# Straight and crossed TensorE quadrants alternating in the chunk inverses of a hybrid decoder kernel

## The chip, the core and the metric

The kernel runs on one core of a Trainium2 chip. The core has TensorE (matrix products; PE in the profile, its weight loads PEld), VectorE (DVE), ScalarE (ACT), GpSimd (POOL) and the DMA queues. Matrix products land in eight banks of PSUM, each 128 partitions by 512 float32. Each time is the device time of one execution in microseconds, and the kernel's time is the median of its runs.

## The reference, cut to what matters

The kernel computes one inference step of a decoder trunk of four layers, for a prompt of 256 tokens and 8 sample sequences of 4 tokens. Layers 0 and 3 have an RWKV-7 time mixer as their token mixer, layer 1 has differential attention, and layer 2 a gated DeltaNet (GDN). In front of each mixer and behind it stands a feed-forward half, which takes most of the time. The mixer's core is this recurrence over the tokens, for 16 heads with 64x64 states:

```python
def step(S, inp):
    r_t, w_t, k_t, v_t, a_t, b_t = inp
    sa = jnp.einsum('bhvk,bhk->bhv', S, a_t)
    S = S * w_t[:, :, None, :] + sa[..., None] * b_t[:, :, None, :] + v_t[..., None] * k_t[:, :, None, :]
    return S, jnp.einsum('bhvk,bhk->bhv', S, r_t)
S, o = lax.scan(step, S0.astype(f32), seq)
```

## The kernel before

The recurrence is not run token by token. The prompt's 256 tokens are cut into four chunks of 64 (c = 0 to 3), and what the tokens of a chunk do to each other is solved by a triangular 64x64 matrix of each head, which has to be inverted. The inverse is built on a ladder of five steps, l = 1 to 5 (LADDER is 6), that doubles the size of the inverted blocks. Each step has two products: Y = (matNT) times the inverse so far, which VectorE multiplies with a mask of 0 and 1 into Yc, and X = (transpose of the inverse) times Yc, which ScalarE copies out as the next inverse. The last step gives the transposed inverse (XTfin) and swaps the operands.

Sixteen heads lie as eight head pairs: the even head of a pair on partitions 0 to 63 (HALVES[0]), the odd one on 64 to 127 (HALVES[1]). A product of 64x64 matrices takes one quadrant of TensorE's array; which one is set by the partitions that it reads and those that it writes. Before, each head reads and writes its own half, so only the two straight quadrants work (0 to 0 and 64 to 64). The head pairs are worked in two groups g of four, q = 0 to 3. Each float32 product stands as two instructions in the trace, so one half of a step (Y or X of both groups) is 8 pairs x 2 heads x 2 = 32 recorded instructions.

What follows what is written out by hand: each engine has its own list of instructions, in the order of the code, and waits on semaphores.

- TensorE (chunk_inverse): Y of g0 and g1 (L1434 in the trace) after inv_ready; then other work of the mixer (spread_inverse L1378 in chunk 0, chunk_output L1505 to L1513 of the chunk before, products of the sample sequences); X of g0 and g1 (L1461, in the last step L1463) after invy_ready and invt_ready; then more such work (transposes L1538 in chunk 0, L1554 and L1562 to L1566 in chunk 2, L1577 and L1585 in chunk 3).
- VectorE (L3128 and around): for each group the transpose of the inverse (turned_inverse, L3072, 32x32 blocks of a 128x256 tile), then the mask (L3111). Beside it stand copies of the samples' states (L3057, L3065), the chunk's outputs (chunk_output, L3207 to L3209) and sample products (L3094 to L3098, L3123 to L3125).
- ScalarE: inverse_out (L2457), for each group one copy from the bank. In step 1 (chunk 1: step 2), behind these, chunk_matrix copies the chunk's matrices out of MK_BANK (L2538, L2540), and counts chunk_a_ready.

The banks, before: X and Y of group g share bank XY_BANK[g] = 0, 1 (X in columns 0 to 255, Y in 256 to 511), and the last step writes XT_BANK = 2, 3. From chunk 1 on, MK_BANK is (2, 3) and MB_BANK (0, 1). So TensorE waits for chunk_a_ready only in front of the last X, which reuses banks 2 and 3.

The gated DeltaNet layer has an inverse of its own (gdn_inverse, L2057 and L2086), in which from step 1 on the products of one pair go to straight and crossed quadrants in turn (L2086), and those of L2057 use two quadrants.

Of the kernel before, what the change touches and what calls it, by code (L numbers as in the profile page):

```python
# [28 lines left out]
LADDER = 6  # L29
# [114 lines left out]
def program(nc, t, stages):  # L144
    f32 = mybir.dt.float32
    ALU = mybir.AluOpType
# [3 lines left out]
    with ctx:  # L150
# [255 lines left out]
        V_BANK, KB_BANK = (0, 4), ((1, 2), (6, 7))  # L406
        MK_BANK, MB_BANK = ((6, 7), (2, 3)), ((3, 0), (0, 1))
        own_inverse = work[:, XM0_, :, :].rearrange("p c n -> p (c n)")
# [7 lines left out]
        X_BANK, Y_BANK, RU_BANK, OS_BANK = (3, 1), (0, 2), (4, 5), (6, 7)  # L416
        XY_BANK, XT_BANK = (0, 1), (2, 3)
        GDN_INVERSES = 2 * (2 * (LADDER - 1) + 2) + 2
# [165 lines left out]
        def out_lo_count(s, w=None, x=None):  # L584

            return out_before(s) + (x + 1 if w is None else CH + w + 1)

        def out_before(s):

            return split_before[s] + {"rwkv": 6, "attn": 3, "gdn": 2}[stages[s][0]] * CH  # L590
# [379 lines left out]
        def _(pe):  # L970
# [430 lines left out]
            def chunk_matrices(c, g):  # L1401
# [10 lines left out]
                last.then_inc(chunk_a_raw, 1)  # L1412

            def chunk_inverse(c, meanwhile, behind):

# [4 lines left out]
                for l in range(1, LADDER):  # L1420
                    for g in range(2):
                        if c or l > 1:
                            after(inv_ready)
                        elif g == 0:
                            after(inv_ready, 2)
                        if l == 1:
                            if c:
                                after(chunk_a_ready)
                            elif g == 0:
                                after(chunk_a_ready, 2)  # L1430
                        for q in range(4):
                            hp = 4 * g + q
                            for r in HALVES:
                                last = nc.tensor.matmul(bank[XY_BANK[g]][r, 256 + 64 * q:320 + 64 * q], matNT[r, hp, :],  # L1434
                                                        invX[r, hp, :], start=True, stop=True)
                        last.then_inc(invy_raw, 1)
# [11 lines left out]
                    for g in range(2):  # L1448
                        after(invy_ready)
                        if l == LADDER - 1 and g == 0:  # L1450
                            after(invt_ready, 2)
                        elif 1 < l < LADDER - 1:
                            after(invt_ready)
                        if c and l == LADDER - 1:
                            after(chunk_a_ready)
                        for q in range(4):
                            hp = 4 * g + q
                            for r in HALVES:
                                y, xt = Yc[r, hp, :], invXT[r, hp, :]
                                if l < LADDER - 1:  # L1460
                                    last = nc.tensor.matmul(bank[XY_BANK[g]][r, 64 * q:64 * q + 64], xt, y, start=True, stop=True)  # L1461
                                else:
                                    last = nc.tensor.matmul(bank[XT_BANK[g]][r, 64 * q:64 * q + 64], y, xt, start=True, stop=True)  # L1463
                        last.then_inc(inv_raw, 1)
# [737 lines left out]
        def _(act):  # L2202
# [130 lines left out]
            def rwkv(s, j):  # L2333
# [121 lines left out]

                def inverse_out(g, dst, ready, banks_):
                    return nc.scalar.copy(dst[:, 4 * g:4 * g + 4], bank[banks_[g]][:, 0:256].rearrange("p (c n) -> p c n", n=64)).then_inc(ready, 1)  # L2457

                for c in range(NCHUNK):
# [22 lines left out]
                    for l in range(1, LADDER - 1):  # L2482
                        if c == 3 and l == 4:
                            new_states(2)
                        for g in range(2):
                            after(inv_raw)
                            inverse_out(g, invX, inv_ready, XY_BANK)
                        if c == 1 and l == 1:
# [25 lines left out]
                    for g in range(2):  # L2514
                        after(inv_raw)
                        inverse_out(g, XTfin, invt_ready, XT_BANK)
                    if c == 1:
# [321 lines left out]
        def _(dve):  # L2839
# [45 lines left out]
            def rwkv(s, j):  # L2885
# [184 lines left out]
                def turned_inverse(g, out, src):  # L3070
                    heads = slice(4 * g, 4 * g + 4)
                    return V.transpose(out[:, heads].rearrange("p c n -> p (c n)"), src[:, heads].rearrange("p c n -> p (c n)"))  # L3072

                for c in range(NCHUNK):
                    f = min(c, 1)
# [9 lines left out]
                    for l in range(1, LADDER):  # L3085
# [18 lines left out]
                        for g in range(2):  # L3104
                            if l > 1:
                                if l == 2 and g == 0:
                                    after(inv_ready, 2 + (GDN_INVERSES if j and c == 0 else 0))
                                after(inv_ready)
                                turned_inverse(g, invXT, invX).then_inc(invt_ready, 1)
                            after(invy_raw)  # L3110
                            TT(Yc[:, 4 * g:4 * g + 4], bank[XY_BANK[g]][:, 256:512].rearrange("p (c n) -> p c n", n=64),  # L3111
                               each4(const(f"block{l}")), ALU.mult).then_inc(invy_ready, 1)
                        if c and l in (2, 3):
# [828 lines left out]
```

## Time and profile before

| | us |
|---|---|
| median of 3 runs (lowest, highest) | 2791.18 (2789.64, 2796.64) |
| the profiled execution's own time | 2788.76 |
| its span, from first to last instruction | 2787.1 |
| TensorE busy | 2730.9 |
| VectorE busy | 1669.9 |
| ScalarE busy | 1238.3 |
| GpSimd busy | 286.0 |

The granted TensorE clock is 0.995 of full speed over the span. The chain of work that ended last is 90% TensorE; the three lines of the feed-forward and projection products alone are 24% each. The ladder's lines L1434, L1461 and L1463 are in the two stretches of the recurrent mixers, at 354 to 486 us and at 2396 to 2528 us. A row of the timeline gives the start, the time from the first start to the last end of the merged instructions, and the engine, line and operation; in brackets stands the idle time in front and what ended it.

### The profile page before, as it was taken

What the parts mean: (1) busy time and instruction counts of PE and PEld (TensorE: products, weight loads), DVE (VectorE), ACT (ScalarE), POOL (GpSimd) and SP (SyncE); (2) the same over time, 40 slices, a digit from 0 to 9 for tenths busy, and PEclk for the clock granted to TensorE, in tenths of its full rate; (3) what the DMA queues carried; (4) which work ended last, traced back from release to release, by engine and by line L of the source; (5) the groups of instructions that cost most, each with busy time, mean ns of one, the idle gap of its engine ahead of it and who ended that gap; (6) DMA issues with size and microseconds to landing.
All of it is one profiled execution on the core that took longest, in us unless ns stands there. A gap on an engine that the chain in (4) does not pass through costs nothing.

```text
span 2787.1 us, 60635 instructions
## 1 busy us (share of the span) xinstructions
PE 2730.9 (98%) x26617; PEld 2579.8 (93%) x26617; DVE 1669.9 (60%) x2529; ACT 1238.3 (44%) x1988; POOL 286.0 (10%) x343
## 2 busy tenths in 40 slices
PE   9999999999999999999999999999999999999999
PEld 8997988999999986999999998789999979788999
DVE  5646866665565546665565594546556558866653
ACT  5435643544444334543443473234344356445443
POOL 2001023000000102000000121410000010122001
PEclk9999999999999999999999999999999999999999
DMA  9444401653653655444653443254455353206442
GB/s 283 132 146 137 139 33 37 190 163 128 198 169 127 245 183 201 143 149 142 187 168 125 155 163 109 69 177 146 144 188 166 127 169 121 63 4 185 151 134 79
DMA packets 351611, 402.47 MB, mean 144 GB/s; under 512 B 31290, under 2 KB 306127, under 8 KB 350989
## 3 DMA queue, kind: packets, MB, share of 16 engines
q1 hardware_dynamic: 340448, 361.73, 40.4%
q0 software_dynamic: 10976, 38.07, 4.4%
q8 instruction: 139, 2.28, 0.3%
q14 instruction: 48, 0.39, 0.0%
HBM read 385.19 MB, written 14.57 MB: 143 GB/s over the span
## 4 chain that ended last, share of the span: by engine, by line
PE 90%; DVE 6%; ACT 2%; issue 1%; DMA 1%; SPq 0%; POOL 0%; DVEq 0%; ACTq 0%; POOLq 0%
PE banks L1018 24%; PE banks L1020 24%; PE banks L1019 24%; PE banks L1461 1%; PE banks L1434 1%; PE banks L1161 1%; PE banks L1008 1%; PE banks L1632 1%; PE banks L1069 1%; PE banks L1585 1%; PE banks L1014 1%; PE banks L1948 1%; DVE ring_lo L2941 1%; PE banks L1409 0%; DVE h L2856 0%
## 5 line engine op out<-in xcount | busy, mean ns | idle before, releaser
L2871 DVE TENSOR_TENSOR w_lo<-ring,w_hi 128x2048 fp32r<-128x2048 f32 (+1 forms) x303 | 609.1, 2010 | 409.5 <-ACT w_hi L2320 409.5
L1018 PE MATMUL banks<-h_hi,w_hi 128*128 128x288 f32 x2816 | 836.9, 297 | 1.1 <-DVE h_lo L2863 0.8
L1019 PE MATMUL banks<-h_hi,w_lo 128*128 128x288 f32 x2816 | 831.5, 295 | 0.0
L1020 PE MATMUL banks<-h_lo,w_hi 128*128 128x288 f32 x2816 | 828.5, 294 | 0.0
L2320 ACT CAST w_hi<-ring 128x2048 fp32r<-128x2048 f32 (+1 forms) x303 | 509.5, 1682 | 573.2 <-PE banks L1020 545.1
L1018 PEld LDWEIGHTS banks<-h_hi,w_hi 128*128 128x128 f32 x2816 | 528.2, 188 | 3.4 <-DVE h_lo L2863 1.9
L1020 PEld LDWEIGHTS banks<-h_lo,w_hi 128*128 128x128 f32 x2816 | 531.0, 189 | 0.0
L1019 PEld LDWEIGHTS banks<-h_hi,w_lo 128*128 128x128 f32 x2816 | 529.1, 188 | 0.4
L1018 PE MATMUL banks<-hid_hi,w_hi 128*128 128x288 f32 x1408 | 416.1, 296 | 0.0
L1019 PE MATMUL banks<-hid_hi,w_lo 128*128 128x288 f32 x1408 | 415.4, 295 | 0.0
L1020 PE MATMUL banks<-hid_lo,w_hi 128*128 128x288 f32 x1408 | 414.3, 294 | 0.0
L1020 PEld LDWEIGHTS banks<-hid_lo,w_hi 128*128 128x128 f32 x1408 | 265.1, 188 | 0.0
L1019 PEld LDWEIGHTS banks<-hid_hi,w_lo 128*128 128x128 f32 x1408 | 264.3, 188 | 0.0
L1018 PEld LDWEIGHTS banks<-hid_hi,w_hi 128*128 128x128 f32 x1408 | 263.8, 187 | 0.0
L2819 ACT CAST hid_hi<-work 128x288 fp32r<-128x288 f32 x176 | 76.2, 433 | 397.9 <-DVE work L3615 397.9
L3671 POOL TENSOR_TENSOR h<-h 128x288 f32<-128x288 f32 x65 | 78.8, 1215 | 1508.8 <-ACT h L2249 902.8
L3607 DVE TENSOR_TENSOR work<-banks,rinv 128x288 f32<-128x288 f32 x176 | 80.5, 457 | 174.0 <-PE banks L1020 174.0
L3617 DVE TENSOR_TENSOR hid_lo<-work,hid_hi 128x288 fp32r<-128x288 f32 x176 | 80.7, 458 | 87.8 <-ACT hid_hi L2819 87.8
L1019 PE MATMUL banks<-h_hi,ring_lo 128*128 128x288 f32 x448 | 132.6, 296 | 0.0
L1019 PEld LDWEIGHTS banks<-h_hi,ring_lo 128*128 128x128 f32 x448 | 84.9, 189 | 0.1
L3630 DVE SCALAR_TENSOR_TENSOR x<-banks,x 128x288 f32<-128x288 f32 x64 | 29.3, 457 | 85.8 <-PE banks L1020 85.8
L3615 DVE TENSOR_TENSOR work<-work 128x288 f32<-128x288 f32 x176 | 79.5, 452 | 1.8 <-ACT work L2817 1.8
(607 smaller groups left out, 4239.9 us busy)
## 6 DMA issues: line engine op xcount, KB each, us to landing
ring<-in_ffn_w_gate SPq DMA_DIRECT2D x87, 1024.0 KB, 5.5
ring<-in_ffn_w_up SPq DMA_DIRECT2D x87, 1024.0 KB, 8.0
ring<-in_ffn_w_down SPq DMA_DIRECT2D x64, 768.0 KB, 4.6
ring<-in_ffn_w_down SPq DMA_DIRECT2D x64, 640.0 KB, 5.8
ring<-in_rwkv_w_rkv SPq DMA_DIRECT2D x24, 1024.0 KB, 6.5
ring<-in_gdn_w_in SPq DMA_DIRECT2D x16, 1024.0 KB, 7.4
ring<-in_attn_w_qkv SPq DMA_DIRECT2D x12, 1024.0 KB, 7.4
ring<-in_rwkv_w_o SPq DMA_DIRECT2D x8, 1024.0 KB, 6.3
```

The lines of the kernel that those rows point to most:

```text
L1008: last = nc.tensor.matmul(bank[at][:, 0:NT], ones[:, :], h[:, c, :], start=(c == 5), stop=(c == 7))
L1018: nc.tensor.matmul(out, w_hi_k, x_hi_k, start=start, stop=False)
L1019: nc.tensor.matmul(out, w_lo_k, x_hi_k, start=False, stop=False)
L1020: return nc.tensor.matmul(out, w_hi_k, x_lo_k, start=False, stop=stop)
L2320: nc.scalar.copy(w_hi[e][:, 0:k, :], raw).then_inc(w_hi_ready, 1)
L2819: nc.scalar.copy(hid_hi[:, 2 * u + e, :], prod[:, e, :]).then_inc(act_hi_ready, 1)
L2871: nc.vector.tensor_tensor(w_lo[e][:, 0:k, :], raw, w_hi[e][:, 0:k, :], ALU.subtract).then_inc(w_lo_ready, 1)
L3607: nc.vector.tensor_tensor(silu[:, e, :], bank[2 * e][:, 0:NT], rinv[:, :], ALU.mult)
L3615: nc.vector.tensor_tensor(prod[:, e, :], silu[:, e, :], prod[:, e, :], ALU.mult).then_inc(prod_ready, 1)
L3617: nc.vector.tensor_tensor(hid_lo[:, f, :], prod[:, e, :], hid_hi[:, f, :], ALU.subtract).then_inc(act_lo_ready, 1)
L3630: nc.vector.scalar_tensor_tensor(x[:, c, :], bank[4 + c % 4][:, 0:NT], 0.5, x[:, c, :], ALU.mult, ALU.add).then_inc(x_updated, 1)
L3671: nc.gpsimd.tensor_tensor(h[:, c, :], h[:, c, :], h[:, other, :], ALU.add).then_inc(presummed, 1)
```

## The change

Half of the head pairs of a group (q = 2 and 3) now run on the crossed quadrants: head e of the pair reads its half and writes the other one in Y; in X it is turned back. They go to banks of their own, CROSS_BANK = 1, 3, while q = 0 and 1 stay in XY_BANK = 0, 2, and the order is q = 0, 2, 1, 3, straight and crossed in turn. It starts at step 2 (chunk 1: step 3, first_crossed); step 1 stays straight in bank XY_BANK[g]. The transposes must follow: for a crossed step each group has three (turned_halves), one for the two straight pairs over all partitions and two for the crossed pairs, from half 0 to half 1 and back. MK_BANK and MB_BANK of the later chunks move, and chunk_a_ready is waited for in front of the first crossed Y.

```diff
-        MK_BANK, MB_BANK = ((6, 7), (2, 3)), ((3, 0), (0, 1))
+        MK_BANK, MB_BANK = ((6, 7), (1, 3)), ((3, 0), (0, 2))
...
-        XY_BANK, XT_BANK = (0, 1), (2, 3)
+        XY_BANK, CROSS_BANK = (0, 2), (1, 3)
+        QUAD_ORDER = (0, 2, 1, 3)
...
+        def first_crossed(c):
+            return 3 if c == 1 else 2
+        def ladder_read(c, l, g, at):
+            if l < first_crossed(c):
+                return bank[XY_BANK[g]][:, at:at + 256].rearrange("p (b n) -> p b n", b=2)
+            return banks[:, XY_BANK[g]:CROSS_BANK[g] + 1, at:at + 128]
...
+            def ladder_out(c, l, g, q):
+                if l < first_crossed(c):
+                    return 0, bank[XY_BANK[g]][:, 64 * q:]
+                return q // 2, bank[(XY_BANK, CROSS_BANK)[q // 2][g]][:, 64 * (q % 2):]
...
+                        elif c and l == first_crossed(c):
+                            after(chunk_a_ready)
-                        for q in range(4):
+                        for q in QUAD_ORDER:
                             hp = 4 * g + q
-                            for r in HALVES:
-                                last = nc.tensor.matmul(bank[XY_BANK[g]][r, 256 + 64 * q:320 + 64 * q], matNT[r, hp, :],
-                                                        invX[r, hp, :], start=True, stop=True)
+                            for i, r in enumerate(HALVES):
+                                at, out = ladder_out(c, l, g, q)
+                                last = nc.tensor.matmul(out[HALVES[i ^ at], 256:320], matNT[r, hp, :], invX[r, hp, :], start=True, stop=True)
...
-                        if c and l == LADDER - 1:
-                            after(chunk_a_ready)
...
+                                y, xt = Yc[HALVES[i ^ at], hp, :], invXT[HALVES[i ^ at], hp, :]
                                 if l < LADDER - 1:
-                                    last = nc.tensor.matmul(bank[XY_BANK[g]][r, 64 * q:64 * q + 64], xt, y, start=True, stop=True)
+                                    last = nc.tensor.matmul(out[r, 0:64], xt, y, start=True, stop=True)
...
+                def turned_halves(g):
+                    own, other = slice(4 * g, 4 * g + 2), slice(4 * g + 2, 4 * g + 4)
+                    flat = lambda a: a.rearrange("p c n -> p (c n)")
+                    V.transpose(flat(invXT[:, own]), flat(invX[:, own]))
+                    for i in range(2):
+                        last = V.transpose(flat(invXT[HALVES[1 - i], other]), flat(invX[HALVES[i], other]))
+                    return last
...
-                                turned_inverse(g, invXT, invX).then_inc(invt_ready, 1)
+                                (turned_inverse(g, invXT, invX) if l < first_crossed(c) else turned_halves(g)).then_inc(invt_ready, 1)
```

The copy of ScalarE and the mask of VectorE read through ladder_read, with as many elements as before.

On VectorE, step 2 of chunk 0, this stood in a row before (the first copy is of the samples' states, STREAM_TRANSPOSE the ladder's transpose, the operation into h the mask):

```order
279 L3057 COPY ring<-banks 128x512 [waits seq_t_raw]
280 L3072 STREAM_TRANSPOSE work<-work 128x256 [waits inv_ready]
281 L3111 TENSOR_TENSOR h<-banks,consts 128x256 [waits invy_raw]
282 L3072 STREAM_TRANSPOSE work<-work 128x256 [waits inv_ready]
283 L3111 TENSOR_TENSOR h<-banks,consts 128x256 [waits invy_raw]
```

And this stands there now:

```order
279 L3075 COPY ring<-banks 128x512 [waits seq_t_raw]
280 L3095 STREAM_TRANSPOSE work<-work 128x128 [waits inv_ready]
281 L3097 STREAM_TRANSPOSE work<-work 64x128 x2
282 L3137 TENSOR_TENSOR h<-banks,consts 128x256 [waits invy_raw]
283 L3095 STREAM_TRANSPOSE work<-work 128x128 [waits inv_ready]
284 L3097 STREAM_TRANSPOSE work<-work 64x128 x2
285 L3137 TENSOR_TENSOR h<-banks,consts 128x256 [waits invy_raw]
```

Each transpose has become three, and the mask stands behind the third.

On TensorE, chunk 2, the end of step 1 (L1554, products of the samples) and Y of step 2 before (ahead of the fillers L1505; some semaphores share a number, so a wait can have another user's name):

```order
1374 L1554 MATMUL banks<-work 64x64 [waits seq_a_ready,pageT_ready_act]
1375 L1554 MATMUL banks<-work 64x64 x15
1376 L1434 MATMUL banks<-work 64x64 [waits inv_ready]
1377 L1434 MATMUL banks<-work 64x64 x7
1378 L1434 MATMUL banks<-work 64x64 [waits inv_ready]
1379 L1434 MATMUL banks<-work 64x64 x7
```

And now:

```order
1374 L1572 MATMUL banks<-work 64x64 [waits seq_a_ready,pageT_ready_act]
1375 L1572 MATMUL banks<-work 64x64 x15
1376 L1454 MATMUL banks<-work 64x64 [waits chunk_a_ready,inv_ready]
1377 L1454 MATMUL banks<-work 64x64 x7
1378 L1454 MATMUL banks<-work 64x64 [waits chunk_a_ready,inv_ready]
1379 L1454 MATMUL banks<-work 64x64 x7
```

The instructions are as many as before and in the same place; both groups now wait for chunk_a_ready, which has gone from the last X.

## Rows read from the trace of the kernel before

**Rows 1.** The page's head.
```profile
span 2787.1 us, 60635 instructions
```

**Rows 2.** Windows of both mixers: busy us by engine, clock, DMA.
```profile
353.96:486.24 132.28, 125.62 (x3307) 109.96 (x3306) 83.79 (x182) 56.45 (x146) 40.86 (x37) 1.00 0.12 27
2395.80:2528.10 132.30, 125.64 (x3307) 109.94 (x3306) 83.81 (x182) 56.48 (x146) 40.85 (x37) 1.00 0.12 27
```

**Rows 3.** Timeline, TensorE, chunk 0: start us, length us, instruction.
```profile
366.33 1.09 PE L1538 MATMUL banks<-consts,ring 128*128 128x128 f32 x8
369.49 1.15 PE L1461 MATMUL banks<-h,work 64*64 64x64 f32 x32
370.57 1.09 PE L1538 MATMUL banks<-consts,ring 128*128 128x128 f32 x8
...
380.34 1.15 PE L1463 MATMUL banks<-work,h 64*64 64x64 f32 x32 [0.50 <-DVE work L3072]
```

**Rows 4.** Timeline, VectorE, chunk 0, step 2.
```profile
367.46 0.69 DVE L3057 COPY ring<-banks 128x512 f32<-128x512 f32 x1 [0.82 <-PE banks L1538]
368.07 0.43 DVE L3072 STREAM_TRANSPOSE work<-work 128x256 f32<-128x256 f32 x1
368.43 0.38 DVE L3111 TENSOR_TENSOR h<-banks,consts 128x256 f32<-128x256 f32 x1
368.74 0.42 DVE L3072 STREAM_TRANSPOSE work<-work 128x256 f32<-128x256 f32 x1
369.09 0.38 DVE L3111 TENSOR_TENSOR h<-banks,consts 128x256 f32<-128x256 f32 x1
```

**Rows 5.** Timeline, TensorE, the GDN inverse.
```profile
1718.82 1.16 PE L2086 MATMUL banks<-work 64*64 64x64 f32 x64
1720.01 1.15 PE L2057 MATMUL banks<-work 64*64 64x64 f32 x32
```

**Rows 6.** VectorE group of one shape: count, busy us, mean ns, idle before.
```profile
L3551 DVE TENSOR_TENSOR work<-work,banks 128x128 f32<-128x128 f32 x2 | 0.5, 284 | 0.0
```

**Rows 7.** Timeline, VectorE, copies between partition halves.
```profile
316.92 0.19 DVE L3013 COPY kinv<-work 128x32 f32<-128x32 f32 x1
317.02 0.77 DVE L3017 COPY kinv<-work 64x32 f32<-64x32 f32 x4
```

**Rows 8.** Timeline, ScalarE and TensorE, chunk 2, step 2.
```profile
422.37 1.10 PE L1434 MATMUL banks<-work 64*64 64x64 f32 x32
422.68 0.37 ACT L2540 COPY work<-banks 128x256 f32<-128x256 f32 x1
...
423.70 0.37 ACT L2540 COPY work<-banks 128x256 f32<-128x256 f32 x1
```

**Rows 9.** Timeline, all engines, chunk 1.
```profile
400.06 2.36 POOL L3691 TENSOR_TENSOR work<-work,consts 128x1024 f32<-128x1024 f32 x1
400.84 1.87 DVE L3209 TENSOR_TENSOR h<-h,kinv 128x256 f32<-128x256 f32 x1
...
404.76 0.67 DVE L3123 TENSOR_TENSOR work<-work,consts 128x512 f32<-128x512 f32 x1
...
410.19 1.10 PE L1463 MATMUL banks<-work,h 64*64 64x64 f32 x32
```

**Rows 10.** Timeline, VectorE and TensorE, chunk 2.
```profile
427.94 0.68 DVE L3094 TENSOR_TENSOR work<-banks,work 128x512 f32<-128x512 f32 x1
...
430.51 1.10 PE L1554 MATMUL banks<-work 64*64 64x64 f32 x32
...
433.66 1.34 PE L1461 MATMUL banks<-h,work 64*64 64x64 f32 x32 [1.12 <-DVE h L3111]
...
438.42 1.15 PE L1463 MATMUL banks<-work,h 64*64 64x64 f32 x32 [0.62 <-DVE h L3111]
```

**Rows 11.** Timeline, VectorE and TensorE, chunk 3.
```profile
453.24 0.69 DVE L3065 COPY ring<-banks 128x512 f32<-128x512 f32 x1 [2.74 <-PE banks L1585]
...
459.38 1.15 PE L1461 MATMUL banks<-h,work 64*64 64x64 f32 x32
```

More of the change, by code:

```diff
@@ L1453, in chunk_inverse @@
                             after(invt_ready)
-                        if c and l == LADDER - 1:
-                            after(chunk_a_ready)
-                        for q in range(4):
+                        for q in QUAD_ORDER:
                             hp = 4 * g + q
-                            for r in HALVES:
-                                y, xt = Yc[r, hp, :], invXT[r, hp, :]
+                            for i, r in enumerate(HALVES):
+                                at, out = ladder_out(c, l, g, q)
+                                y, xt = Yc[HALVES[i ^ at], hp, :], invXT[HALVES[i ^ at], hp, :]
                                 if l < LADDER - 1:
-                                    last = nc.tensor.matmul(bank[XY_BANK[g]][r, 64 * q:64 * q + 64], xt, y, start=True, stop=True)
+                                    last = nc.tensor.matmul(out[r, 0:64], xt, y, start=True, stop=True)
                                 else:
-                                    last = nc.tensor.matmul(bank[XT_BANK[g]][r, 64 * q:64 * q + 64], y, xt, start=True, stop=True)
+                                    last = nc.tensor.matmul(out[r, 0:64], y, xt, start=True, stop=True)
                         last.then_inc(inv_raw, 1)
@@ L2454, in new_states, with inverse_out @@
                     nc.scalar.copy(dst[:, 0], bank[4 + 2 * (p // 2)][:, :].rearrange("p (q b k) -> p b q k", q=2, b=4)).then_inc(seq_new_ready, 1)
-                def inverse_out(g, dst, ready, banks_):
-                    return nc.scalar.copy(dst[:, 4 * g:4 * g + 4], bank[banks_[g]][:, 0:256].rearrange("p (c n) -> p c n", n=64)).then_inc(ready, 1)
+                def inverse_out(c, l, g, dst, ready):
+                    return nc.scalar.copy(dst[:, 4 * g:4 * g + 4].rearrange("p (b q) n -> p b (q n)", b=2), ladder_read(c, l, g, 0)).then_inc(ready, 1)
                 for c in range(NCHUNK):
@@ L2486, in rwkv @@
                             after(inv_raw)
-                            inverse_out(g, invX, inv_ready, XY_BANK)
+                            inverse_out(c, l, g, invX, inv_ready)
                         if c == 1 and l == 1:
@@ L2515, in rwkv @@
                         after(inv_raw)
-                        inverse_out(g, XTfin, invt_ready, XT_BANK)
+                        inverse_out(c, LADDER - 1, g, XTfin, invt_ready)
                     if c == 1:
@@ L3108, in rwkv @@
                                 after(inv_ready)
-                                turned_inverse(g, invXT, invX).then_inc(invt_ready, 1)
+                                (turned_inverse(g, invXT, invX) if l < first_crossed(c) else turned_halves(g)).then_inc(invt_ready, 1)
                             after(invy_raw)
-                            TT(Yc[:, 4 * g:4 * g + 4], bank[XY_BANK[g]][:, 256:512].rearrange("p (c n) -> p c n", n=64),
-                               each4(const(f"block{l}")), ALU.mult).then_inc(invy_ready, 1)
+                            TT(Yc[:, 4 * g:4 * g + 4].rearrange("p (b q) n -> p b q n", b=2),
+                               ladder_read(c, l, g, 256).rearrange("p b (q n) -> p b q n", n=64),
+                               each4(const(f"block{l}")).rearrange("p (b q) n -> p b q n", b=2), ALU.mult).then_inc(invy_ready, 1)
                         if c and l in (2, 3):
```

## The prediction

> **What bounds the kernel now.** I read four things in this order: the span and the windows of the two recurrent mixers, the timeline of one ladder step with its waits, one place elsewhere in the kernel that already uses crossed quadrants, and the rows that price narrow VectorE instructions. The reader is to see this. The profiled execution took 2788.76 us with a span of 2787.1 us [rows 1]; it is 2.4 us below the median of the runs, 2791.18, so I make the sum on 2788.76 and add 2.4 at the end. TensorE is busy for 2730.9 us of it. The change touches only the two mixer stretches of 132.3 us each [rows 2]; in each, TensorE is busy for 125.6 us and VectorE for 83.8 us, at full clock. The two stretches agree within 0.02 us, so I work one and double it. Outside them TensorE goes on bound by its own products, so a shift in a mixer should reach the end whole.
>
> Names used below: a ladder step l has two halves on TensorE, Y (the products of matNT and X) and X (the products of Yc and the transpose). Each half is 8 head pairs in two groups g0, g1, 32 recorded instructions. VectorE does for each group a transpose T and then a mask M; ScalarE copies X out. "Last start" is when the last instruction of a half starts.
>
> One step of chunk 0 shows who ends last. TensorE runs transposes L1538, Y, spread L1378, X, transposes again: from 366.33 to 370.57, 4.24 us, with no idle time in front of any of them [rows 3]. VectorE runs copy L3057, T, M, T, M from 367.46, and its last M starts at 369.09 [rows 4]; X starts right behind the end of that M, 369.47. So TensorE bounds, with VectorE's chain only just hidden. That is the cover which the change spends.
>
> **Part 1: TensorE, quicker halves.** A half of 32 instructions takes 1.15 us from first start to last end, straight quadrants only [rows 3]. The GDN inverse has halves in which straight and crossed pairs alternate: 64 instructions took 1.16 us, beside 1.15 us for its own 32-instruction halves that use two quadrants [rows 5]. So twice the instructions fit in the same time. A recorded instruction lasts 0.218 us and the first after a wait 0.267 us, so the 32 starts spread over 0.93 us, 0.058 us for two; with four quadrants it is 0.058 us for four, 0.47 us in all. A crossed half saves 0.47 us. Chunks 0, 2 and 3 have 4 crossed steps (8 halves), chunk 1 has 3 (6 halves): 30 halves, 14.0 us in a mixer, if nothing else is late. The ScalarE copies and the masks keep their sizes (they read two banks in place of one): I cost that at nothing, since the element counts do not change; if the step from bank to bank took 0.01 us, the 22 masks that my chains have on the path in a mixer would make 0.4 us in both.
>
> **Part 2: VectorE, three transposes in place of one.** For each group of a crossed step one 128x256 transpose becomes one 128x128 and two 64x128. No row shows a transpose of that width. Bounds: at 128 columns a mask-like operation takes 0.284 us, against 0.384 for the same kind at 256 columns [rows 4, 6], 0.10 to 0.13 less, so a narrow transpose is about 0.31 us from 0.43; at the most, it costs as much as the wide one. At the least, consecutive operations overlap by 0.07 us (T to M starts 0.36 apart at a duration of 0.43 [rows 4]), so 0.24 apart.
>
> What decides is whether they overlap. The second reads half 0 and writes half 1, the third the reverse, and M goes back to half 0. Just such a sequence stands in the trace [rows 7]: L3013 takes 0.19 us and the next operation starts 0.10 us behind its start, but the four copies of L3017, each going to or from other partition halves, take 0.77 us together. Less one duration of 0.19, that is 0.19 to 0.20 us from start to start: they do not overlap at all. So I take 0.32 us from start to start three times, 0.96 us from T to M, where 0.36 stood: 0.60 us more for a group, 1.2 us for a step. Bounds for T to M: 3 x 0.24 = 0.72 us and 3 x 0.45 = 1.35 us.
>
> The Trainium skill has a rule for this ("VectorE: DVE Perf Modes", section Two Vector instructions with no wait between them): an instruction whose input or output starts in another 32-partition quadrant than the last one's is held until every earlier Vector instruction has finished. It speaks against this change; by it all three steps (second, third, M) are held, and the trace agrees at L3017. Without it T to M would be 0.72 us.
>
> **Part 3: a wait moved forward.** Crossed results go to banks 1 and 3, where the chunk's own matrices lie until ScalarE has copied them. So chunk_a_ready is now waited for at the first crossed step, and not at the last. In chunk 2 that is l=2: Y started at 422.37, but ScalarE ends the copies of g0 at 423.05 and of g1 at 424.07 [rows 8]. g1 starts at 424.12 and its last instruction at 424.35, in place of 423.30: 1.05 us later where 0.47 earlier was to be had, a cost of 1.5. Queued behind it on TensorE is all the rest. In chunk 1 (l=3) the same order of copies costs 1.2 us. In chunk 3 other matmuls stand between, and the copies are done in time: nothing.
>
> **The sum by chunk, start to start.** From the start of the first T to the last start of X there are 0.96 + 0.31 + 0.96 to the second M, 0.42 for that M (it no longer overlaps), and 0.33 until the last instruction of g1's X: 2.98 us. Where VectorE decides, I follow this chain.
>
> - Chunk 0. At l=2 T starts at 368.07 as now; X's last start is 371.05, where it is 370.42 (369.49 + 0.93): +0.6. Then a loop: 0.15 to L1538, 1.16 to L3057, 0.61 to T, 2.98: 4.9 us, against 4.24: +0.7 for l=3. Step 4 now takes 3.8 (it has a shorter spread): +1.1. Step 5: 0.8 us of VectorE work stands between M and T, and it takes 3.35 from last start to last start, where X (380.34 [rows 3]) shows 2.8: +0.6. Together +3.0.
> - Chunk 1. VectorE's L3209 lasts until 402.71 beside GpSimd work that ends at 402.42 [rows 9], and this end stays. T at 402.7; M of g0 waits for Y to 403.8, second M at 405.1, then 0.31 and three products of 0.64 (L3123 [rows 9] and its two like), T 407.3, X's last start 410.3. It is 411.1 now (410.19 + 0.88): -0.8. The 2.8 us of part 1 have paid for the wait and for this.
> - Chunk 2. L3094 at 427.94 [rows 10] stays too, as L3209 before it again ends with GpSimd's work. T at 428.55, X's last start 431.53, where it is 430.46, just ahead of L1554 at 430.51: +1.1. L1554 follows 1.1 later; 1.15 us behind its start L3097, 1.21 us for it and the next, then 2.98: X's last start 436.9 against 434.8 (433.66 + 1.12): +2.2. The fillers and the copy before the last T take 2.45 as now, X's last start 442.4 against 439.35 (438.42 + 0.93): +3.0.
> - Chunk 3. T at 453.85 (L3065 at 453.24 + 0.61 [rows 11]), X 456.8; chunk_output's three operations follow the mask (1.4 us), T at 457.5, X's last start 460.5 against 460.31 (459.38 + 0.93 [rows 11]): +0.2. The last four halves have long matmuls between them and save 0.47 each, 1.9, less 0.4 us where g1 waits for its mask at l=4: -1.3.
>
> Together 3.0 - 0.8 + 3.0 - 1.3 = +3.9 us a mixer, +7.8 us in two. 2788.8 + 7.8 + 2.4 = 2799.0 us. The clock stays at its upper level (2.4 GHz, 1.00 granted): no wait that I add is longer than 1.5 us, and idle times of 1.1 us stand in chunk 2 now [rows 10] at full clock.
>
> **Rivals.**
>
> (a) The transposes overlap after all (0.24 apart, 0.72 from T to M). For it: a transpose and the mask behind it overlap now [rows 4]. Against it: the copies of [rows 7]. The same chains give +0.6, -1.4, +1.1 and -2.9: -2.6 us a mixer, 2786 us.
>
> (b) A narrow transpose costs what the wide one costs (1.35 from T to M). That is 0.78 us more in each of about 11 steps that VectorE then bounds: 8.6 us a mixer more, 3.9 + 8.6 = 12.5, twice, 2816 us. For it: no row has the width. Against it: all other kinds get cheaper with fewer columns.
>
> (c) TensorE remains the bound, and VectorE's growth hides in its idle 48 us of each stretch. 14.0 us less the moved wait of 2.7: 11.3 a mixer, 2769 us, faster. For it: the shares in [rows 2]. Against it: T, M, T, M stand in a row between two halves, and there the cover is 0 in chunk 0. It needs T to M at no more than about 0.5 us.
>
> (d) The quadrants do not overlap here, so the change does not do what it says: halves stay at 1.15 us and VectorE's part comes on top. About 7.8 us a mixer of the saved halves that my sum uses would be gone: 11.7 twice, 2814 us. Against it: [rows 5], with the same sizes and the same alternation.
>
> **How the numbers follow.** About 8.4 us, 0.3%, is what a measurement of this kernel can tell from no change. My forecast of 7.8 lies at that border: its own range is 2793 to 2804, as the 0.31 us of a narrow transpose is uncertain by 0.02, which is worth 2.5 us in all, and the chains by some 3. It has 0.62 (0.31 slower, 0.31 same); (a) 0.13, within 0.3%; (b) 0.10, slower; (c) 0.08, faster; (d) 0.03, slower; 0.04 for what I have not named, faster for the most part. Slower 0.44, same 0.44, faster 0.12. The range reaches below (a) and nearly to (b): 2782 to 2815.
>
> **What would show it.** Right: 64*64 halves of the ladder with last starts 0.44 behind the first where nothing is waited for; transposes of about 0.31 us whose starts lie 0.32 apart; T to M near 0.96; TensorE idle of 0.5 to 1.5 us before X in chunks 0 and 2, put down to the masks; chunk 0 longer by 3 us, chunk 3 shorter by 1.3; Y at the first crossed step of chunk 2 waiting for ScalarE's L2540 copies. Wrong: transposes that overlap, or of 0.43 us; idle time before X on TensorE no longer than now; or a difference that arises outside the two stretches.

## The result and the profile after

The changed kernel takes 2810.53 us (median of 4 runs, 2809.76 to 2814.87), beside 2790.41 us for the kernel before in the same comparison: the ratio is 1.007, with a 95% interval of 1.0058 to 1.0082. That is 20.1 us more. The forecast was 2799.0 us, 7.8 us more. The sign was right and the time lies inside the range of 2782 to 2815, but the difference is 2.6 times the one worked out. The page of the profiled execution (2809.76 us) begins:

```profile
span 2808.1 us, 60761 instructions
```

All of it arises in the two mixer stretches. These are their windows, cut at the same instructions as [rows 2] (span, busy us of PE, PEld, DVE, ACT and POOL, granted clock, DMA share, GB/s):

```profile
353.83:496.35 142.52, 120.91 (x3306) 102.91 (x3306) 97.00 (x241) 56.07 (x145) 40.69 (x37) 0.95 0.11 25
2406.49:2550.11 143.62, 121.46 (x3306) 103.93 (x3306) 96.98 (x241) 56.07 (x145) 40.69 (x37) 0.94 0.10 24
```

They are 10.24 and 11.32 us longer than the 132.28 and 132.30 of before, 21.6 in all; the profiled executions differ by 21.0. VectorE is busy for 13.2 us more in each (97.00 against 83.79), as three transposes stand for one. And the last columns have something new: the clock is at 0.95 and 0.94 of full speed, where it was at 1.00.

Step 2 of chunk 0 on VectorE, which answers to [rows 4] (start us, length us, instruction):

```profile
367.33 0.69 DVE L3075 COPY ring<-banks 128x512 f32<-128x512 f32 x1 [0.81 <-PE banks L1556]
367.94 0.30 DVE L3095 STREAM_TRANSPOSE work<-work 128x128 f32<-128x128 f32 x1
368.26 0.63 DVE L3097 STREAM_TRANSPOSE work<-work 64x128 f32<-64x128 f32 x2
368.92 0.43 DVE L3137 TENSOR_TENSOR h<-banks,consts 128x256 f32<-128x256 f32 x1
369.26 0.30 DVE L3095 STREAM_TRANSPOSE work<-work 128x128 f32<-128x128 f32 x1
369.57 0.62 DVE L3097 STREAM_TRANSPOSE work<-work 64x128 f32<-64x128 f32 x2
370.23 0.42 DVE L3137 TENSOR_TENSOR h<-banks,consts 128x256 f32<-128x256 f32 x1
```

From the start of T to the start of M it is 0.98 us, where 0.36 stood. The same step on TensorE, for [rows 3]:

```profile
366.20 1.09 PE L1556 MATMUL banks<-consts,ring 128*128 128x128 f32 x8
367.23 0.69 PE L1454 MATMUL banks<-work 64*64 64x64 f32 x32
367.85 1.12 PE L1389 MATMUL banks<-work,consts 128*128 128x512 f32 x2
369.40 0.46 PE L1479 MATMUL banks<-h,work 64*64 64x64 f32 x16 [0.42 <-DVE h L3137]
370.71 0.46 PE L1479 MATMUL banks<-h,work 64*64 64x64 f32 x16 [0.85 <-DVE h L3137]
```

A crossed half that waits for nothing (L1454) takes 0.69 us instead of 1.15, so the quadrants do overlap. But X (L1479) now comes in two pieces, each behind the mask of its group, with 0.42 and 0.85 us of idle time that VectorE ends. Before, the time in front of X was zero.

What I had not forecast stands in these windows of the changed kernel (same columns), the four stretches of low clock that lie in the mixers' ladders:

```profile
383.50:386.90 3.40, 3.29 (x72) 3.08 (x76) 1.70 (x4) 0.95 (x3) 3.32 (x2) 0.50 0.02 5
441.50:451.70 10.20, 7.93 (x177) 7.54 (x178) 5.97 (x12) 1.15 (x4) 5.21 (x5) 0.50 0.01 3
2434.90:2441.70 6.80, 5.44 (x112) 5.23 (x116) 3.31 (x9) 1.90 (x4) 4.62 (x4) 0.50 0.01 2
2496.30:2506.50 10.20, 8.32 (x183) 7.93 (x184) 4.70 (x12) 1.90 (x4) 6.02 (x5) 0.50 0.01 3
```

The granted clock is 0.50, the lower of its two levels (1.2 GHz), for 30.6 us in all. In the kernel before it is 1.00 throughout both ladders. In chunk 2, TensorE's rows then read:

```profile
440.57 0.46 PE L1479 MATMUL banks<-h,work 64*64 64x64 f32 x16 [2.24 <-DVE h L3137]
...
441.89 0.71 PE L1479 MATMUL banks<-h,work 64*64 64x64 f32 x16 [0.85 <-DVE h L3137]
442.37 1.86 PE L1580 MATMUL banks<-consts,work 64*64 64x32 f32 x32
444.04 1.79 PE L1584 MATMUL banks<-work 64*64 64x32 f32 x30
...
445.71 1.14 PE L1454 MATMUL banks<-work 64*64 64x64 f32 x30
448.73 1.13 PE L1481 MATMUL banks<-work,h 64*64 64x64 f32 x32 [1.88 <-DVE work L3097]
449.79 1.97 PE L1397 MATMUL banks<-consts,work 128*64 128x64 f32 x32
```

The instructions of L1580, L1584 and L1397 took 1.07, 1.10 and 1.15 us before, and a crossed half (L1454) takes 0.69 us at the upper level.

I read the shift of the ladder from the timelines: the last start of a half in the changed kernel less that in the kernel before, both counted from the mixer's first Y (362.62 against 362.75 in the first mixer, 2415.28 against 2404.59 in the second). The last columns are of the run with fillers, below.

| last start of | forecast | changed, mixer 1 | mixer 2 | filled, mixer 1 | mixer 2 |
|---|---|---|---|---|---|
| chunk 0, last X | +3.0 | +3.30 | +3.29 | +3.29 | +3.29 |
| chunk 1, first Y | +3.0 | +4.33 | +5.39 | +3.29 | +3.29 |
| chunk 1, last X | +2.2 | +4.29 | +5.06 | +3.28 | +2.79 |
| chunk 2, first Y | +2.2 | +4.56 | +5.05 | +3.61 | +3.71 |
| chunk 2, last X | +5.2 | +10.33 | +10.38 | +7.35 | +6.75 |
| chunk 3, first Y | +5.2 | +11.02 | +12.09 | +7.12 | +6.52 |
| chunk 3, last X | +3.9 | +10.24 | +11.32 | +6.35 | +5.74 |

### The profile page after: what moved, and what is told of

It is laid out like the page before. It is cut to its first block, busy times and chain, and to the rows that moved or that the text cites. A ratio compares the mean times of both kernels' runs of the same rounds, so it can differ in the third digit from the quotient of the medians.

```text
span 2808.1 us, 60761 instructions
## 1 busy us (share of the span) xinstructions
PE 2721.6 (97%) x26617; PEld 2566.3 (91%) x26617; DVE 1697.0 (60%) x2649; ACT 1237.4 (44%) x1988; POOL 285.9 (10%) x343
## 4 chain that ended last, share of the span: by engine, by line
PE 87%; DVE 8%; ACT 3%; issue 1%; DMA 1%; SPq 0%; POOL 0%; DVEq 0%; ACTq 0%; POOLq 0%
PE banks L1029 24%; PE banks L1031 24%; PE banks L1030 23%; DVE work L3097 1%; PE banks L1172 1%; PE banks L1479 1%; DVE h L3137 1%; PE banks L1019 1%; PE banks L1420 1%; PE banks L1650 1%; PE banks L1497 1%; PE banks L1025 1%; PE banks L1966 1%; PE banks L1603 1%; PE banks L1080 1%
```

## The experiments

My theory after the result: (1) transposes that change the partition half are held, so VectorE's chain grows by 0.6 us for a group and TensorE waits for it; (2) the moved wait costs its forecast 2.7 us a mixer; (3) TensorE's clock falls behind the idle time of (1) and (2), which the forecast left out. The rivals are that the number or width of the transposes is the cost, that crossed quadrants or the banks are, and that the low clock lies where VectorE bounds anyway and costs nothing.

### Three flat transposes

```diff
+                def turned_thrice(g):
+                    for a, b in ((0, 96), (96, 192), (192, 256)):
+                        last = V.transpose(flat(invXT)[:, a:b], flat(invX)[:, a:b])
```

> The kernel before with each transpose of the later ladder steps cut into three that all start at partition 0 (96, 96 and 64 of the 256 columns); TensorE untouched. My theory (three narrow instructions cost mainly because a change of the partition half lets none overlap): here they overlap, start to start 0.20 us, the mask starts 0.55 to 0.60 us behind the first transpose where it was 0.36, and the time is 4 to 8 us over before. Rival (three instructions cost what they cost whatever halves they use): the mask 0.9 us behind and 15 us or more over before.

Measured: 2793.34 us, beside 2791.28 for before; ratio 1.0008 [0.9998, 1.0017]. Its VectorE at step 2 of chunk 0:

```profile
367.66 0.56 DVE L3077 STREAM_TRANSPOSE work<-work 128x96 f32<-128x96 f32 x3
368.14 0.39 DVE L3117 TENSOR_TENSOR h<-banks,consts 128x256 f32<-128x256 f32 x1
```

The mask starts 0.48 us behind the first transpose (0.36 before; the transposes are 0.250 us long at 96 columns in the mean, 0.203 at 64), where I expected 0.55 to 0.60. A mixer's ladder grows by 0.9 us. I expected 4 to 8 us over before and got 2, which the interval does not tell from no change; the number of transposes alone is not the cost.

### The three transposes of the change, quadrants straight

The kernel before, with turned_halves in place of turned_inverse in the later steps, and nothing else.

> The kernel before with the changed kernel's three transposes in the same steps, TensorE's products straight as before (so half of the pairs get the other half's transpose: the ladder is left wrong). It has VectorE's price alone. My theory: 0.96 us from the first transpose to the mask, about 9 us a mixer from the added VectorE time and some more where TensorE's clock falls to its lower level behind the idle time: 20 to 30 us over before, more than the changed kernel. Rival (what slows the changed kernel lies in the crossed products or the moved wait): under 8 us over before.

Measured: 2813.26 us, ratio 1.0074 [1.0054, 1.0094], as slow as the whole change. T to M is 0.97 us again (368.40 to 369.37). The ladders grow by 11.1 us each, of it 3.7 in chunk 0, nothing in chunk 1, 2.6 in chunk 2 up to X of step 4; then the clock falls here too:

```profile
442.10:452.30 10.20, 9.22 (x168) 8.82 (x169) 4.51 (x10) 1.83 (x4) 6.03 (x5) 0.50 0.02 3
```

So neither crossed quadrants nor the banks are needed for the low clock; VectorE's part alone can bring it. In chunk 0 of this kernel it did not fall. It need not fall in each execution either: three of the four took 2813.06 to 2813.54 us at a mean granted clock of 0.991, the fourth 2806.23 us at 0.995, and only one of the three is traced.

### The change with one transpose

```diff
-  (turned_inverse(g, invXT, invX) if l < first_crossed(c) else turned_halves(g))
+  turned_inverse(g, invXT, invX)
```

> The changed kernel with one 128x256 transpose for each group, as before (so the crossed pairs get a transpose of the wrong half): TensorE's gain and the moved wait, without VectorE's price. My theory: crossed halves in 0.47 us, chunk 3 shorter by 3 us, the clock stays up, and the time is 18 to 25 us under before. Rival (quadrants do not run side by side here): no faster than before.

Measured: 2787.88 us, ratio 0.9987 [0.9977, 0.9997]. This was a miss: 3.4 us under the kernel before, not 18 to 25. The ladders are 5.0 and 2.9 us shorter, 7.9 in all. The profiled execution (2789.82 us) does not keep this: from the end of the first mixer's ladder to the start of the second's it needs 8.5 us more than that of before, and there the clock fell in a stretch that the edit does not touch and in which TensorE is busy throughout (last row below; 1.00 in the kernel before). The ten executions lie between 2779.74 us (mean clock 0.996) and 2791.47 (0.993), so the median says less of the ladders than their rows do; why the clock falls outside them, no run shows. Chunk 0 shows why the ladders gain no more:

```profile
369.42 0.95 PE L1479 MATMUL banks<-h,work 64*64 64x64 f32 x32
369.46 0.39 DVE L3137 TENSOR_TENSOR h<-banks,consts 128x256 f32<-128x256 f32 x1
```

X starts behind the first mask, and its second group has to wait for the second one, which starts at 369.46: the half takes 0.95 us, not 0.69. In the first mixer chunk 0 gains 2.1 us of the 3.6 that eight halves could give; chunk 1 gains 1.4, chunk 2 loses 0.8, mostly by the moved wait, 0.4 more goes between chunks 2 and 3, and chunk 3 gains 2.7. In the second mixer the clock fell for 6.8 us at 2480.1. The windows are the same stretch of both mixers, up to there, and the stretch of low clock outside:

```profile
418.80:434.80 16.00, 11.99 (x447) 10.86 (x446) 10.23 (x23) 4.68 (x14) 3.59 (x2) 1.00 0.02 4
2464.10:2480.10 16.00, 11.71 (x440) 10.73 (x436) 10.73 (x23) 5.09 (x15) 3.59 (x2) 1.00 0.02 4
1575.50:1589.10 13.60, 13.60 (x147) 11.95 (x147) 5.60 (x25) 3.47 (x13) 0.15 (x1) 0.50 0.01 1
```

TensorE is about equally thin in both mixers, but the clock fell behind this stretch only in the second. So quicker halves and the moved wait, without VectorE's price, can bring the low clock too, and behind a thin stretch it need not come. Even transposes at the old price leave VectorE's T, M, T, M as the bound: rival (c) of the prediction, 11.3 us a mixer, had no room here.

### Banks, order and wait only

```diff
-                return q // 2, bank[(XY_BANK, CROSS_BANK)[q // 2][g]][:, 64 * (q % 2):]
+                return 0, bank[(XY_BANK, CROSS_BANK)[q // 2][g]][:, 64 * (q % 2):]
```

This stands on top of the last edit: straight quadrants, one transpose.

> The changed kernel with straight quadrants and one transpose: what is left is the order of pairs, the banks and the wait for the chunk's matrices at the first crossed step. My theory: g1 of that step starts 1.0 us later in chunk 1 and 1.3 us later in chunk 2, part of it is caught again, and nothing else moves: 2 to 5 us over before. Rival (the wait is hidden by other work): within 1 us of before; rival (reads over two banks are dearer): copies and masks longer than 0.37 and 0.38 us.

Measured: 2796.11 us, ratio 1.0017 [1.0006, 1.0027], 4.8 us over. The ladders grow by 2.5 and 2.8 us, in the first mixer only at two places: 1.15 us at the first Y with the wait in chunk 1, 1.35 us (the shift goes from 1.15 to 2.58, and settles at 2.50) at that of chunk 2, where TensorE shows:

```profile
424.83 0.84 PE L1454 MATMUL banks<-work 64*64 64x64 f32 x16 [0.66 <-ACT work L2558]
425.85 0.35 PE L1454 MATMUL banks<-work 64*64 64x64 f32 x5 [0.19 <-ACT work L2558]
```

In the second mixer they are 1.22 and 1.43. That is the wait of part 3, priced at 1.2 and 1.5 us in the prediction, where the price includes the 0.45 us that a crossed half would have given. Masks and copies across two banks cost nothing that shows.

### The idle time filled

```diff
+                    if c == 0 and l > 1:
+                        after(seq_t_ready_act, 1, keep=False)
+                        keep_clock(4, 2 if l > 3 else 1)
+                    if c == 2 and l > 3:
+                        after(chunk_state_ready, 2, keep=False)
+                        keep_clock(6, 2)
```

Filler products in front of X, whose results nobody reads; VectorE's instructions are those of the changed kernel.

> The changed kernel with filler products on TensorE (128x512, into banks that hold nothing at that point) in the idle time in front of X at the crossed steps of chunk 0 and at steps 4 and 5 of chunk 2. VectorE's work and order stay. Theory (about 8 of the 20 us come from TensorE's clock, which falls behind this idle time): the granted clock of the windows 384.7 to 393.7 and 437.6 to 458.7 goes from 0.88, 0.66 and 0.89 back to about 1.00, X's last starts inside chunk 0 stay where they are in the changed kernel (+3.3 us), the start of chunk 3 goes from +11 to about +8 us, and the run is 6 to 10 us below the changed kernel, 10 to 14 us above the kernel before. Rival (the low clock only lies beside work that VectorE bounds): clock back up, but the time stays within 2 us of the changed kernel, 18 to 22 us above the kernel before. Second rival (fillers do not hold the clock up): clock still 0.50 in parts of these windows, time unchanged.

Measured: 2805.68 us (2802.5 to 2807.61), beside 2791.48; ratio 1.0051 [1.0037, 1.0064]. That is 14.2 us over, where the changed kernel is 20.1 over. Its mixers, cut as above:

```profile
353.47:492.10 138.63, 124.86 (x3326) 101.78 (x3326) 97.08 (x241) 55.97 (x145) 40.67 (x37) 1.00 0.11 25
2404.71:2542.77 138.06, 124.72 (x3326) 101.81 (x3326) 97.19 (x241) 56.11 (x145) 40.72 (x37) 1.00 0.11 25
```

The clock is back at 1.00, and the stretches are 3.9 and 5.6 us shorter than in the changed kernel, though TensorE does more work. At the end of chunk 0:

```profile
381.67 1.98 PE L1025 MATMUL banks<-consts 128*128 128x512 f32 x4
383.58 0.69 PE L1487 MATMUL banks<-work,h 64*64 64x64 f32 x32
384.21 1.15 PE L1397 MATMUL banks<-consts,work 128*64 128x64 f32 x32
```

The fillers (L1025) stand where 1.51 us of idle time stood, the last X takes 0.69 instead of 1.13 us, and L1397 behind it 1.15 instead of 1.97. Inside chunk 0 X's last starts are those of the changed kernel (+3.29), so the fillers cost nothing there. Both rivals fall: fillers hold the clock up, and the low clock had a price. By the medians it is 5.9 us, just under the 6 to 10 expected; by the windows of the profiled executions 9.5. The profiled execution is the fastest of the five (mean clock 0.997, the others 0.993 and 0.994), and the others have no trace. The intervals of the two ratios overlap slightly, so the medians alone leave the clock's share between nearly nothing and some 10 us; that the clock was restored in the traced execution, and the time of these stretches with it, is plain in the rows.

### Which transpose is held

Three kernels for single instructions. In the first, both transposes of a group go from the lower half to the lower half:

> The changed kernel, but in the crossed steps VectorE issues for a group two transposes of 64x128, both from the lower partition half to the lower one; the upper half is left out. For the reading of single instructions, not for the time. Theory (an instruction is held when its input or output starts in another partition half than the last one's): these do not change the half, so the second starts about 0.23 us behind the first (0.30 less the 0.07 by which consecutive operations overlap), and the mask 0.23 behind the second: 0.46 from T to M. Rival (what keeps them apart is that only 64 partitions are used): 0.32 apart, 0.64 from T to M.

```profile
368.52 0.49 DVE L3096 STREAM_TRANSPOSE work<-work 64x128 f32<-64x128 f32 x2
368.93 0.38 DVE L3136 TENSOR_TENSOR h<-banks,consts 128x256 f32<-128x256 f32 x1
```

The mask starts 0.41 us behind the first transpose (0.46 expected), the second transpose 0.225 us behind it: they overlap, though each uses only 64 partitions (one time, 2786.22 us). In the second, the change's three shapes, each half turned in place:

> The changed kernel with the same three shapes of transposes (128x128, 64x128, 64x128), but each half turned in place, lower to lower and upper to upper: the crossed pairs get the wrong halves. Theory (held at a change of half): the second does not change the half and starts 0.23 us behind the first, the third (upper half) and the mask (all partitions again) are held, 0.32 each: 0.87 from T to M, 0.09 less for a group than in the changed kernel, about 1.5 us less in a mixer where VectorE's chain ends last, so 2 to 5 us below the changed kernel. Rival (shape alone): 0.96 from T to M, time unchanged.

```profile
367.33 0.30 DVE L3095 STREAM_TRANSPOSE work<-work 128x128 f32<-128x128 f32 x1
367.56 0.58 DVE L3097 STREAM_TRANSPOSE work<-work 64x128 f32<-64x128 f32 x2
368.17 0.42 DVE L3137 TENSOR_TENSOR h<-banks,consts 128x256 f32<-128x256 f32 x1
```

The first transpose of 64x128 starts 0.23 us behind the one before it, where it is 0.32 in the changed kernel; the last (upper half) and the mask start only behind the end of the one before them, as there. T to M is 0.84 us (0.87 expected), and the kernel takes 2805.9 us (beside 2789.28; ratio 1.0062 [1.0045, 1.0079]), 16.6 over instead of 20.1, as expected. In the third, the 128x128 transpose comes last:

> The changed kernel with the three transposes of a group in another order: the two between the halves first, the 128x128 one last. Theory: the first is now held behind the operation before it (0.43 us from the start of the mask of 0.42 us, where 0.34 stands in the changed kernel), the third too, and the mask is not: 0.87 from T to M, 0.09 less, and 0.09 more from M to the next T. Time unchanged within 3 us. Rival (64-partition instructions hold what follows them, whatever it is): T to M 0.96 or more less nothing before it.

```profile
368.15 0.62 DVE L3096 STREAM_TRANSPOSE work<-work 64x128 f32<-64x128 f32 x2
368.79 0.31 DVE L3097 STREAM_TRANSPOSE work<-work 128x128 f32<-128x128 f32 x1
369.02 0.39 DVE L3136 TENSOR_TENSOR h<-banks,consts 128x256 f32<-128x256 f32 x1
369.44 0.63 DVE L3096 STREAM_TRANSPOSE work<-work 64x128 f32<-64x128 f32 x2
```

Now the mask starts 0.23 us behind the last transpose, not held, and the next T starts 0.42 behind the mask, held, where it was 0.34. T to M is 0.87, and the time (2808.98 us, one run) is the changed kernel's. The hold sits exactly where the starting half changes, and reordering only moves it.

### Crossed where it is covered

Crossed quadrants only at steps 4 and 5 of chunk 1 and steps 3 to 5 of chunk 3:

```diff
-        def first_crossed(c):
-            return 3 if c == 1 else 2
+        def crossed(c, l):
+            return (c, l) in ((1, 4), (1, 5), (3, 3), (3, 4), (3, 5))
```

The wait for the chunk's matrices moves with them: to step 4 in chunk 1, step 3 in chunk 3 and Y of the last step in chunk 2.

> The changed kernel, but crossed quadrants, the three transposes and the banks of their own only in the last two steps of chunk 1 and the last three of chunk 3, where the idle time of TensorE in the kernel before or long matmuls between the halves cover VectorE's 0.6 us more for a group; all other steps as in the kernel before. Theory (the change pays only where VectorE's chain does not end last, and each of these halves saves up to 0.47 us): 0.5 to 2 us less a mixer, 1 to 4 us below the kernel before in all, which is hardly to be told from no change; clock in both mixers as in the kernel before. Rival (banks and order cost wherever they are used, as in the run with straight quadrants, and the three transposes hold sample_state's work up): 2 to 6 us above the kernel before.

Measured: 2785.71 us (2781.38 to 2788.28, 7 runs), beside 2791.48; ratio 0.9973 [0.9962, 0.9985]. It is 5.8 us faster than the kernel before, more than the 1 to 4 expected, and the fastest of the three. Its mixers:

```profile
356.12:485.61 129.49, 122.69 (x3273) 106.93 (x3274) 87.23 (x200) 56.23 (x145) 39.30 (x35) 0.99 0.10 22
2396.86:2526.94 130.08, 122.53 (x3306) 106.72 (x3306) 88.87 (x201) 56.21 (x145) 40.91 (x37) 1.00 0.11 27
```

They are 2.8 and 2.2 us shorter than [rows 2]. Of these, 0.9 and 0.8 come in chunk 1 and 1.5 in chunk 3; the other 0.4 of the first mixer lies ahead of the first crossed step, so it is none of the edit's. That makes 4.6 us by the windows, where I had expected 0.5 to 2 a mixer. A half whose cover holds gives back 0.45 us, as at step 4 of chunk 1 (shift from 0.01 to -0.45 in the second mixer), but the next half often gives nothing, for it waits for VectorE; ten such halves could have given 4.5 a mixer.

## Why the prediction came out as it did

- **Part 1, quicker halves: right.** Last starts came 0.45 us earlier than before wherever nothing was waited for (0.47 forecast), and the half takes 0.69 us. Rival (d) is out.
- **Part 2, the transposes: right.** 0.302 us for 128x128 and 0.306 for 64x128 (0.31), 0.315 and 0.319 from start to start (0.32), T to M 0.98 (0.96). Only M to the next T was low, 0.34 where the sum had 0.31. Rivals (a) and (b) are out. The rule of the Trainium skill that I weighed ("VectorE: DVE Perf Modes", section Two Vector instructions with no wait between them) compares the quadrants in which inputs and outputs start; by it, the second transpose of the run with halves turned in place is not held, and neither is the mask behind a last 128x128. The trace agrees at both places, with 0.23 us from start to start in place of 0.32 and 0.34.
- **Part 3, the wait: right, a little low.** 1.15 and 1.35 us measured alone. As the prediction counts it, with the 0.45 us not gained, the shift at that Y of the first mixer is 1.37 in chunk 1 (from +4.33 to +5.25) and 1.66 in chunk 2 (from +4.56 to +5.77), where I had 1.2 and 1.5.
- **The sum at full clock: too low by 4.3 us.** The filled kernel shows +6.35 and +5.74, where I had +3.9 each. In the first mixer the 2.45 us are 0.3 in chunk 0, 0.8 in chunk 1, 0.3 between chunks 1 and 2, 0.7 in chunk 2 and 0.3 in chunk 3; in the second, 1.84, chunk 1 takes 0.3, chunk 2 comes out as forecast and the step between chunks 1 and 2 takes 0.9. The 0.3 of chunk 0 is four steps with T to M at 0.98 twice and M to T at 0.34. Part of chunk 1 can be told too. My anchor held: VectorE's L3236 (L3209 before) ends at 406.92 in the changed kernel, just where 402.71 lands when the ladder is 4.2 us later (the 4.33 of the table, less 0.13 by which this mixer starts earlier). But I let the mask behind it wait for Y to 403.8, and it waited longer:

```profile
405.94 0.98 DVE L3236 TENSOR_TENSOR h<-h,kinv 128x256 f32<-128x256 f32 x1
...
406.58 1.45 PE L1564 MATMUL banks<-ring 128*64 128x64 f32 x32
...
408.48 0.43 DVE L3137 TENSOR_TENSOR h<-banks,consts 128x256 f32<-128x256 f32 x1 [0.70 <-PE banks L1454]
```

  408.48 less 4.2 is 404.3, 0.5 later than my 403.8. About 0.3 of this is the moved wait, whose 0.9 us had not been paid back by then: "The 2.8 us of part 1 have paid for the wait" spent savings of halves that come only later, or that a mask swallows. The rest is in the first mixer only, where L1564 in front of this Y takes 1.45 us; in the second it takes 1.15, as before, and the mask is 0.3 late. Why L1564 is longer there, and what makes the shift between chunks 1 and 2, stays open.
- **The step that failed: "The clock stays at its upper level (2.4 GHz, 1.00 granted): no wait that I add is longer than 1.5 us, and idle times of 1.1 us stand in chunk 2 now [rows 10] at full clock."** The clock did not stay up. I looked at single idle times, one by one, and at a stretch in which TensorE was otherwise full. The change does not add one pause, it thins out whole stretches: quicker halves and a pause in front of each X together. The windows of chunk 0, first of the changed kernel, up to where the clock falls, then of the kernel before, show it:

```profile
353.83:383.40 29.57, 21.42 (x461) 15.32 (x460) 24.87 (x60) 9.66 (x24) 8.68 (x11) 1.00 0.10 38
```

```profile
353.00:384.70 31.70, 29.03 (x601) 22.52 (x602) 24.15 (x52) 12.82 (x32) 13.09 (x12) 1.00 0.13 47
```

  TensorE is busy for 21.42 us of 29.57, where it was busy for 29.03 of 31.70; the clock is still at 1.00 in this stretch, and at 0.50 right behind it. In chunk 2 it falls in the second of two idle times, of 2.24 and 0.85 us, with half a half (0.46 us) between them, and 2.24 is also more than the 1.5 that I had allowed. That such a thin stretch is what makes the clock fall is argued from these rows and from the filled kernel. It is not a rule that forecasts the fall: with one transpose, the same stretch at about the same share fell in one mixer and not in the other. The price was 3.9 and 5.6 us in the two mixers of the traced executions, about half of the 20 us (5.9 us by the medians). With it and the 4.3 us above, 7.8 becomes 21.6, the growth of the windows.

That the range held was luck: 2810.5 us lies outside my forecast's own 2793 to 2804, and the wide range owed its upper end to rival (b), with 2816 us, not to any case that named the clock.

## What to carry to other kernels

When TensorE is the bound and its work gets quicker beside a chain of another engine that was only just hidden, most of the gain is lost (with transposes at the old price and the wait moved, the ladders were 5.0 and 2.9 us shorter, where 30 quicker halves could have given 13.5 each), and what the change adds to that chain counts almost in full; sort the steps by how much cover each has, and apply it only where there is some (here 5 of the 15 crossed steps of a mixer, which turned +20 us into -6). When a change makes TensorE pause in every loop, forecast its busy share over the whole stretch, look in the trace for the clock behind stretches as thin as that, not only for pauses as long, and give the low clock a chance and a price of its own; where it falls, idle time can be filled with products that nobody reads. On VectorE, several small instructions are cheap (three flat transposes cost 0.12 us more than one) as long as they don't change the partition half from one to the next.

## What the runs showed of the hardware

- TensorE's granted clock went to 0.50 for 3.4 to 10.2 us at a time behind stretches in which it paused before each X; the same 32 products took 1.97 us instead of 1.15. It did so with straight quadrants too, and not where fillers stood in the pauses (one traced execution of each kernel). With one transpose it fell in one mixer (11.71 us of TensorE work in the 16.00 before) and stayed up at the same place of the other (11.99 in 16.00). In that execution it was 0.50 for 13.6 us in a stretch in which TensorE had no idle time.
- Transposes of 32x32 blocks on VectorE took 0.43 to 0.45 us at 256 columns, 0.302 at 128, 0.250 at 96 and 0.203 at 64, and at 64 partitions by 128 columns 0.306 when held and 0.26 to 0.29 when not: partitions hardly matter, columns do.
- A VectorE instruction behind one with the same starting half began 0.07 to 0.09 us before that one's recorded end, and 0.01 to 0.03 us behind it where the half changed. The mask took 0.42 us when held and 0.38 to 0.39 when not.
- Straight and crossed quadrants in turn started four 64x64 products in the time of two: the 32 starts of a half spread over 0.48 us, on the two straight ones over 0.93.
